# Moving GpSimd's work and the small state products of a chunked scan, and cutting the last weight loads

## Chip, cores and metric

The kernel runs on one core of one Trainium2 chip. The metric is device time in microseconds (us). The 3 runs of the kernel before gave 721.09, 721.67 and 723.37 us; the median is 721.67 us.

## What is computed

One decoder layer on 512 tokens of width 1024, in float32. One input projection feeds a state space group (16 heads, the scan below) and an attention group (16 heads with a forget gate); both are normalised, projected back and added to the input. Then a mixture of 32 gated experts follows, two for each token. Cut to what matters:

```python
proj = rmsnorm(x, norm_mix_w) @ w_in
z, xbc, dt, q, k, v, f = ...             # column ranges of proj
xbc = silu(causal_dwconv(xbc))           # X, B, C
# scan, in 4 chunks of 128 tokens
a = dt * A;  cum = cumsum(a)             # inside a chunk
decay  = exp(causal(cum_t - cum_s))
y_diag = einsum((C.B) * decay * dt, X)
states = einsum(B, exp(cum_end - cum), X * dt)
h      = exp(cum_end) * h + states       # from chunk to chunk
y_off  = einsum(C, h_in) * exp(cum)
y_ssm  = rmsnorm((y_diag + y_off + X * d_skip) * silu(z))
q, k   = rmsnorm(q), rmsnorm(k)          # per head
y_att  = rmsnorm(softmax(q.k + c_t - c_s) @ v)
x = x + concat(y_ssm, y_att) @ w_out
x = x + moe(rmsnorm(x))                  # top group of 4, 2 of its 8 experts
# expert: (silu(x@w_gate) * (x@w_up)) @ w_down, width 256
```

## The kernel before

Each engine has a program of its own, written out by hand, and semaphores tie them. TensorE (PE), VectorE (DVE), ScalarE (ACT), GpSimd (POOL) and SyncE (SP, which issues DMAs) each work through their list in order.

The projections are 60 passes of TensorE. A pass has 8 tiles (k = 0 to 7), each of 3 float32r products of 128x512, since each float32 factor is split into a high and a low part (`three`, L1402 to L1404). A block of 512 weight columns is used by four passes in a row. Its slots are loaded by SP into a ring of 6 (`raw`), ACT makes the high part (`high`), DVE the low part (`weight_low`, L282, here "a low"); SP loads a slot when the low of the slot six before is made. Seven lows follow the third pass of a block and one the fourth.

The scan runs beside the 16 passes of the q and k columns. The text counts these passes i = 0 to 15; chunk c of the scan belongs to passes 4c to 4c+3. The names:

- ACT, for each pass i: the square of the pass's result, an `Ln` and an `Exp` for the row norm, the copy of a transposed tile. After pass 4c: the copy of the products C.B (`cb_copy`), two groups of decays (`decays`, L1138, four heads each) and for c > 0 the exponential of `decay_out` (L1144), the decays on the outgoing side; after pass 4c+1 the other two groups.
- DVE, for each pass i: a sum and a scaling (`qk_sum`, `qk_scale`, L2067). After pass 4c, `m_product` of groups 0 and 1, after 4c+1 of groups 2 and 3 (L2080); then `y_add(c, 0)` and after pass 4c+2 `y_add(c, 1)` (L2089 to L2099), and after pass 4c+3 `state_keep` for both halves.
- PE: `diag(c, w)` (L1521, four products), `y_off(c, g)` (L1543), `state(c, g)` (L1556), `cb(c)` (L1531) and the transposes `qk_transpose` (L1563) stand between tiles and passes. `diag(c, 2)` writes the bank that `y_add(c, 0)` has to read out first (`y_diag`).
- POOL: the mask of the decays (`causal_decays`), `scaled_x` (X times decay, for `state`), `gate` (y times silu(z)) and `skip_term` (X times d_skip, put into `y`). One tile `y` serves all chunks: `skip_term(c+1)` works on what SP loads into `y` once `gate(c)` has read it.
- SP: `load_conv_chunk(c)` waits for `gated` of chunk c-1 and loads `y`; right behind it in SP's list stands `load_decay_out(c)`, two loads of 256 KB into `decay_out`.

The experts come in 16 pairs of two. For each pair SP streams 6 MB of weights (`gu`, `dn`). PE turns the tokens, does the gate and up products (`gate_up`, L1784, L1807, L1813), a transpose and the down products (`down`, L1842, in two column halves of 512 and two row parts q = 0, 1). The result of the last pair is added to sums that POOL gathers from the output (`gather_last_sums`) and scattered. `keep_busy(n)` are n products of constants whose result nobody reads.

## Time and profile before

| what | value |
|---|---|
| median of 3 runs | 721.67 us |
| profiled execution, its own time | 722.29 us |
| its span | 720.6 us |
| PE busy | 679.8 us (94%) |
| PE weight loads | 470.5 us (65%) |
| DVE busy | 389.4 us (54%) |
| ACT busy | 291.4 us (40%) |
| POOL busy | 132.3 us (18%) |
| mean DMA rate over the span | 226 GB/s |
| mean granted TensorE clock | 0.976 |

The span is what the profiler saw of one execution; 1.7 us of its own time lie around it. Busy PE means that a product was under way, not that it ran at its peak. In rows of the profile, "idle before <-" names what ended an engine's idle time. The passes of q and k run from about 137 to 258 us, attention to about 415 us, and the expert weights stream from about 486 us at 400 to 424 GB/s until about 705 us.

### The profile page before, as it was taken

What the parts mean: (1) busy time and instruction counts of PE and PEld (TensorE: products, weight loads), DVE (VectorE), ACT (ScalarE), POOL (GpSimd) and SP (SyncE); (2) the same over time, 40 slices, a digit from 0 to 9 for tenths busy, and PEclk for the clock granted to TensorE, in tenths of its full rate; (3) what the DMA queues carried; (4) which work ended last, traced back from release to release, by engine and by line L of the source; (5) the groups of instructions that cost most, each with busy time, mean ns of one, the idle gap of its engine ahead of it and who ended that gap; (6) DMA issues with size and microseconds to landing.
All of it is one profiled execution on the core that took longest, in us unless ns stands there. A gap on an engine that the chain in (4) does not pass through costs nothing.

```text
span 720.6 us, 10643 instructions
## 1 busy us (share of the span) xinstructions
PE 679.8 (94%) x3850; PEld 470.5 (65%) x3850; DVE 389.4 (54%) x845; ACT 291.4 (40%) x651; POOL 132.3 (18%) x167
## 2 busy tenths in 40 slices
PE   8999999999999999999999999989999978878975
PEld 7878888777777888767767788877434323323542
DVE  6866678878879665777887643471222211212211
ACT  5934534465555546665676423221212111202200
POOL 2300010114222120022223110020132321122331
PEclk9999999999999999999999999979999989989998
DMA  8333255426254343191020079689999999999993
GB/s 297 95 115 117 77 175 162 131 74 176 82 153 146 88 146 104 45 362 46 19 100 2 10 291 424 241 335 376 412 417 416 403 409 399 424 418 414 412 403 120
DMA packets 61159, 162.77 MB, mean 226 GB/s; under 512 B 14184, under 2 KB 25604, under 8 KB 49840
## 3 DMA queue, kind: packets, MB, share of 16 engines
q1 hardware_dynamic: 49120, 144.64, 53.6%
q0 software_dynamic: 6880, 9.02, 4.3%
q10 hardware_dynamic: 5104, 8.39, 3.2%
q8 instruction: 33, 0.54, 0.3%
q14 instruction: 22, 0.18, 0.1%
HBM read 157.67 MB, written 20.28 MB: 247 GB/s over the span
## 4 chain that ended last, share of the span: by engine, by line
PE 27%; DMA 9%; SPq 9%; DVE 2%; issue 2%; ACT 1%; POOL 0%; POOLq 0%; DVEq 0%; ACTq 0%
PE bank L1813 6%; DMA s_gu<-in_w_expert_gate_dram 4%; SPq L427 4%; DMA s_gu<-in_w_expert_up_dram 4%; PE bank L1842 3%; PE bank L1402 3%; PE bank L1404 3%; PE bank L1403 3%; SPq L475 2%; SPq L461 2%; PE bank L1784 2%; PE bank L1678 1%; PE bank L1635 1%; PE bank L1618 1%; PE bank L1760 1%
## 5 line engine op out<-in xcount | busy, mean ns | idle before, releaser
L1813 PE MATMUL bank<-s_gu,s_xgT 128*64 128x512 f32 x352 | 84.6, 636 | 15.8 <-DMA s_gu<-in_w_expert_up_dram 15.8
L282 DVE TENSOR_TENSOR s_wl<-s_raw,s_wh 128x512 fp32r<-128x512 f32 x116 | 91.6, 836 | 11.8 <-ACT s_wh L1019 11.5
L1019 ACT ACTIVATE s_wh<-s_raw 128x512 fp32r<-128x512 f32 x120 | 72.6, 627 | 42.1 <-PE bank L1404 18.6
L1402 PE MATMUL bank<-s_wh,s_hTh 128*128 128x512 f32 x192 | 78.7, 410 | 0.0
L1404 PE MATMUL bank<-s_wh,s_hTl 128*128 128x512 f32 x192 | 75.2, 391 | 0.0
L1403 PE MATMUL bank<-s_wl,s_hTh 128*128 128x512 f32 x192 | 74.8, 390 | 0.0
L1813 PEld LDWEIGHTS bank<-s_gu,s_xgT 128*64 128x64 f32 x352 | 28.4, 146 | 70.9 <-issue 70.9
L1318 ACT ACTIVATE s_sg<-bank,s_slot_scale 128x256 f32<-128x256 f32 x16 | 7.6, 474 | 151.7 <-PE bank L1813 104.5
L1842 PE MATMUL bank<-s_dn,s_hidT 128*64 128x512 f32 x256 | 58.5, 598 | 1.6 <-DVE s_hidT L2385 1.6
L2385 DVE COPY s_hidT<-bank 128x256 f32<-128x256 f32 x16 | 6.8, 424 | 92.9 <-PE bank L1822 92.9
L2418 DVE SCALAR_TENSOR_TENSOR s_yrow<-bank,s_slot_scale,s_xg 128x512 f32<-128x512 f32 x30 | 21.2, 746 | 46.4 <-PE bank L1842 46.4
L1402 PEld LDWEIGHTS bank<-s_wh,s_hTh 128*128 128x128 f32 x192 | 36.1, 188 | 10.1 <-issue 2.8
L895 POOL DMA_INDIRECT s_xg<-x_rows,s_slot_rows x16 | 16.6, 1038 | 140.0 <-DVE s_yrow L2418 105.3
L1404 PEld LDWEIGHTS bank<-s_wh,s_hTl 128*128 128x128 f32 x192 | 36.0, 188 | 7.9
L1403 PEld LDWEIGHTS bank<-s_wl,s_hTh 128*128 128x128 f32 x192 | 36.1, 188 | 7.5 <-issue 0.7
L1402 PE MATMUL bank<-s_hTh,s_wh 128*128 128x512 f32 x96 | 39.2, 409 | 0.0
L1404 PE MATMUL bank<-s_hTh,s_wl 128*128 128x512 f32 x96 | 37.7, 392 | 0.0
L1403 PE MATMUL bank<-s_hTl,s_wh 128*128 128x512 f32 x96 | 37.4, 389 | 0.0
L1842 PEld LDWEIGHTS bank<-s_dn,s_hidT 128*64 128x64 f32 x256 | 17.0, 136 | 31.2 <-issue 27.1
L1190 ACT ACTIVATE s_Pe<-s_Pe,s_nmax 128x512 f32<-128x512 f32 (+3 forms) x41 | 22.6, 554 | 25.1 <-DVE s_nmax L2167 25.1
L2039 DVE SCALAR_TENSOR_TENSOR s_acc<-s_up,s_cvec,s_acc 128x512 f32<-128x512 f32 x36 | 28.7, 797 | 1.3
L775 POOL TENSOR_SCALAR_AFFINE_SELECT s_decay_rows<-s_decay_rows 128x2048 f32<-128x2048 f32 x4 | 8.5, 2121 | 107.2 <-DMA s_decay_rows<-decay_rows 107.2
(307 smaller groups left out, 1372.2 us busy)
## 6 DMA issues: line engine op xcount, KB each, us to landing
s_dn<-in_w_expert_down_dram SPq DMA_DIRECT2D x28, 1024.0 KB
s_gu<-in_w_expert_gate_dram SPq DMA_DIRECT2D x26, 1024.0 KB
s_gu<-in_w_expert_up_dram SPq DMA_DIRECT2D x24, 1024.0 KB, 30.2
s_raw<-in_w_in_dram SPq DMA_DIRECT2D x88, 256.0 KB, 4.4
s_raw<-in_w_out_dram SPq DMA_DIRECT2D x32, 256.0 KB, 3.4
s_gu<-in_w_expert_up_dram SPq DMA_DIRECT2D x12, 512.0 KB
s_decay_rows<-decay_rows SPq DMA_DIRECT2D x4, 1024.0 KB, 4.6
s_gu<-in_w_expert_gate_dram SPq DMA_DIRECT2D x8, 512.0 KB
```

Source lines behind the costliest of these rows:

```text
L282: eng.tensor_tensor(low, full, high.bitcast(F32), ALU.subtract).then_inc(sem(f"{what}_low_{low_engine(what, i)}"), 1)
L427: sp.dma_start(m[f"gu{b}"][:, half, which, :, :].rearrange("p k f -> p (k f)"), src).then_inc(sem(f"gu_in{b}"), 16)
L895: pool.indirect_dma_start(out=token_rows(p), out_offset=None, in_=x2_dram[:, :], in_offset=bass.IndirectOffsetOnAxis(ap=slot_rows[:, p:p + ...
L1019: act.activation(wh[:, i % HL, :], raw[:, i % RAW, :], ACT.Copy).then_inc(sem("w_high"), 1)
L1190: act.activation(p_tile(v), p_tile(v), ACT.Exp, bias=nmax[:, v:v + 1], scale=-1.0, accum_out=rsum[:, v:v + 1]).then_inc(sem("p_exp"), 1)
L1402: pe.matmul(dst, ah, bh, start=start, stop=False)
L1403: pe.matmul(dst, ah, bl, start=False, stop=False)
L1404: return pe.matmul(dst, al, bh, start=False, stop=stop)
L1813: last = pe.matmul(ps[j][r, :].rearrange("p (w f) -> p w f", w=2), m["xgT"][:, j, k, r], gu[:, half, :, k, :], start=(k == 0), stop=(k == ...
L1842: last = pe.matmul(ps[6 + nb][r, :], m["hidT"][:, j, at:at + CAP], dn[:, half, q, nb * BLK:(nb + 1) * BLK], start=(q == 0), stop=(q == 1))
L2039: ins = dve.scalar_tensor_tensor(out=a, in0=up[:, f % 2, t:t + T], scalar=tap[t], in1=a, op0=ALU.mult, op1=ALU.add)
L2418: dve.scalar_tensor_tensor(out=m["yrow"][:, j, cols], in0=ps[6 + nb][:], scalar=gates, in1=token_rows(p)[:, cols], op0=ALU.mult, op1=ALU.a ...
```

## The change

Five edits in the scan and three at the end:

- PE: the first `cb(0)` stands two tiles later. `diag(c, 0)` and `diag(c, 1)` stand behind tiles 2 and 4 of pass 4c+2 (before: 1 and 3). `diag(c, 2)` and `diag(c, 3)`, which stood side by side at the boundary behind pass 4c+2, stand behind tiles 1 and 3 of pass 4c+3, and `y_off(c, 1)` behind tile 4 of it.
- POOL: `skip_term(c + 1)` stands ahead of `scaled_x(c + 1)`. `scaled_x(c)` waits for the chunk's last `m_product`. `gate(c)` waits for `state_keep(c, 1)`, and in the last chunk for the last `qk_sum`.
- DVE: the copies of `y` onto itself in chunk 0 are gone (`y_diag` of chunk 0 takes the place of `y_whole`, whose counts fall by 2), and the scaling of `dte` stands behind the first two `m_product`.
- ACT: the first square stands ahead of the table load, and the two exponentials for `dte` and `etot` behind the first decays.
- SP: the counts of `y_whole` follow; no load moves in its list.
- End: `keep_busy(5)` stands between the down products of pair 14 and the gate products of pair 15; the second row part of the last down weights comes as four loads of 256 KB (columns 0 to 511 of both experts, then 512 to 1023) instead of two of 512 KB, and the last down product of all waits for the last two alone (`last_columns_in`).

```diff
@@ load_last_down
-            for q in range(2):
+            for half in range(2):
+                src = w_expert_down[0][p + half * NPAIR].rearrange("(p k) n -> p k n", p=P)[:, 0, :]
+                sp.dma_start(m[f"dn{p % NDN}"][:, half, 0, :], src).then_inc(sem(f"dn_in{p % NDN}"), 16)
+            for nb in range(2):
+                cols = slice(nb * BLK, (nb + 1) * BLK)
                 for half in range(2):
-                    src = w_expert_down[0][p + half * NPAIR].rearrange("(p k) n -> p k n", p=P)[:, q, :]
-                    sp.dma_start(m[f"dn{p % NDN}"][:, half, q, :], src).then_inc(sem("last_down_in" if q else f"dn_in{p % NDN}"), 16)
+                    src = w_expert_down[0][p + half * NPAIR].rearrange("(p k) n -> p k n", p=P)[:, 1, cols]
+                    sp.dma_start(m[f"dn{p % NDN}"][:, half, 1, cols], src).then_inc(sem("last_columns_in" if nb else "last_down_in"), 16)
@@ load_decay_out, load_first_bias
-                sp.wait_ge(sem("y_whole"), 2 * c)
+                if c == 1:
+                    sp.wait_ge(sem("y_diag"), 2)
+                else:
+                    sp.wait_ge(sem("y_whole"), 2 * (c - 1))
...
-                sp.wait_ge(sem("y_whole"), 2 * TC)
+                sp.wait_ge(sem("y_whole"), 2 * (TC - 1))
@@ POOL
                 if c < TC - 1:
+                    pool.wait_ge(sem("m_done"), 4 * c + 4)
                     if c:
                         pool.wait_ge(sem("state_done"), 2 * c)
...
-                pool.wait_ge(sem("y_whole"), 2 * c + 2)
+                if c:
+                    pool.wait_ge(sem("y_whole"), 2 * c)
+                else:
+                    pool.wait_ge(sem("y_diag"), 2)
+                if c < TC - 1:
+                    pool.wait_ge(sem("state_kept"), 2 * c + 2)
+                else:
+                    pool.wait_ge(sem("qk_sum"), 16)
...
                 gate(c)
+                skip_term(c + 1)
                 scaled_x(c + 1)
-                skip_term(c + 1)
@@ ACT
+            qk_square(0)
             act.preload_act_table_set("natural_log_exp_and_others")
-            act.wait_ge(sem("steps_known"), 4)
-            act.activation(dte[:], dte[:], ACT.Exp).then_inc(sem("dt_acts"), 1)
-            act.activation(etot[:], tot[:, :, 0:H], ACT.Exp).then_inc(sem("dt_acts"), 1)
...
                     if i:
                         decay_out_exp(i // 4)
+                    else:
+                        act.wait_ge(sem("steps_known"), 4)
+                        act.activation(dte[:], dte[:], ACT.Exp).then_inc(sem("dt_acts"), 1)
+                        act.activation(etot[:], tot[:, :, 0:H], ACT.Exp).then_inc(sem("dt_acts"), 1)
@@ PE
-                    if i == 1 and k == 1:
+                    if i == 1 and k == 3:
                         cb(0)
-                    if i >= 2 and i % 4 == 2 and k in (1, 3):
-                        diag(i // 4, k // 2)
+                    if i >= 2 and i % 4 == 2 and k in (2, 4):
+                        diag(i // 4, k // 2 - 1)
+                    if i >= 2 and i % 4 == 3 and k in (1, 3):
+                        diag(i // 4, 2 + k // 2)
+                    if i > 4 and i % 4 == 3 and k == 4:
+                        y_off(i // 4, 1)
...
-                if step == 1:
-                    if c:
-                        y_off(c, 1)
-                    diag(c, 2)
-                    diag(c, 3)
...
+                    elif final and q:
+                        pe.wait_ge(sem("last_columns_in"), 32)
...
                 down(p, p)
+                if p == NPAIR - 2:
+                    keep_busy(5)
@@ DVE
-                else:
-                    dve.tensor_copy(y[:, cols], y[:, cols]).then_inc(sem("y_whole"), 1)
...
-                if i == 0:
-                    dve.wait_ge(sem("dt_acts"), 5)
-                    dve.tensor_tensor(dte[:], dte[:], sp[:, :, 0:H], ALU.mult).then_inc(sem("scales_known"), 1)
-                    dve.wait_ge(sem("scales_known"), 1)
...
                     m_product(c, 1)
+                    if c == 0:
+                        dve.wait_ge(sem("dt_acts"), 5)
+                        dve.tensor_tensor(dte[:], dte[:], sp[:, :, 0:H], ALU.mult).then_inc(sem("scales_known"), 1)
+                        dve.wait_ge(sem("scales_known"), 1)
```

What stands in a row on POOL from the mask of chunk 1 to the gating of chunk 1, before (`s_decay_rows` the mask, `s_zs` the gating, `s_Xs` the scaled X, `s_y` the skip term):

```order
L763 TENSOR_TENSOR s_Xs<-s_X,s_dte 128x1024 [waits x_silu,x_rows,scales_known]
L775 AFFINE_SELECT s_decay_rows<-s_decay_rows 128x2048 [waits cum_rows_moved]
L770 TENSOR_TENSOR s_zs<-s_y,s_zs 128x1024 [waits z_stored,y_whole]
L763 TENSOR_TENSOR s_Xs<-s_X,s_dte 128x1024 [waits state_done]
L755 TENSOR_TENSOR s_y<-s_y,s_dskip_of 128x1024 [waits conv_chunk_in]
L775 AFFINE_SELECT s_decay_rows<-s_decay_rows 128x2048 [waits cum_rows_moved]
```

and now:

```order
L771 TENSOR_TENSOR s_Xs<-s_X,s_dte 128x1024 [waits x_silu,m_done,x_rows,scales_known]
L790 AFFINE_SELECT s_decay_rows<-s_decay_rows 128x2048 [waits cum_rows_moved]
L785 TENSOR_TENSOR s_zs<-s_y,s_zs 128x1024 [waits z_stored,state_kept,y_diag]
L762 TENSOR_TENSOR s_y<-s_y,s_dskip_of 128x1024 [waits conv_chunk_in]
L771 TENSOR_TENSOR s_Xs<-s_X,s_dte 128x1024 [waits state_done,m_done]
L790 AFFINE_SELECT s_decay_rows<-s_decay_rows 128x2048 [waits cum_rows_moved]
```

The skip term moved ahead of the scaled X, the gating waits for the kept state, and the scaled X for the m products.

What stands on TensorE behind pass 4c+2 of chunk 1, before (`s_qn` the transpose, `s_BC,s_Hst` is `y_off`, `s_M,s_X` is `diag`, the 512 wide ones are tiles of the pass):

```order
L1563 MATMUL bank<-s_ident,s_qn 128x128 x3
L1543 MATMUL bank<-s_BC,s_Hst 128x128 [waits state_kept,y_off_scaled]
L1543 MATMUL bank<-s_BC,s_Hst 128x128 x3
L1521 MATMUL bank<-s_M,s_X 64x128 [waits y_diag,m_done]
L1521 MATMUL bank<-s_M,s_X 64x128 x3
L1521 MATMUL bank<-s_M,s_X 64x128 [waits m_done]
L1521 MATMUL bank<-s_M,s_X 64x128 x3
L1402 MATMUL bank<-s_wh,s_hTh 128x512 [waits qk_scaled]
L1403 MATMUL bank<-s_wl,s_hTh 128x512
```

and now, the tiles left out where a line of dots stands:

```order
L1581 MATMUL bank<-s_ident,s_qn 128x128 x3
L1420 MATMUL bank<-s_wh,s_hTh 128x512 [waits qk_scaled]
...
L1422 MATMUL bank<-s_wh,s_hTl 128x512
L1539 MATMUL bank<-s_M,s_X 64x128 [waits y_diag,m_done]
L1539 MATMUL bank<-s_M,s_X 64x128 x3
L1420 MATMUL bank<-s_wh,s_hTh 128x512
...
L1539 MATMUL bank<-s_M,s_X 64x128 [waits m_done]
L1539 MATMUL bank<-s_M,s_X 64x128 x3
...
L1561 MATMUL bank<-s_BC,s_Hst 128x128 [waits state_kept,y_off_scaled]
L1561 MATMUL bank<-s_BC,s_Hst 128x128 x3
L1420 MATMUL bank<-s_wh,s_hTh 128x512
```

The two groups of `diag` and the `y_off` left the boundary and stand alone among the tiles of the pass behind it.

## Rows read from the trace of the kernel before

**Rows 1.** The chain that ended last (start us, us, what), its last long transfer.
```profile
667.26 31.48 DMA s_gu<-in_w_expert_gate_dram
```

**Rows 2.** TensorE's waits: line, who, us in total, times, longest.
```profile
PE bank L1521 <- DVE s_y L2089: 0.8, 1, 0.8
PE bank L1563 <- DVE s_qn L2067: 0.7, 1, 0.7
PE bank L1521 <- DVE s_M L2080: 0.6, 1, 0.6
PE bank L1531 <- ACT s_BC L1085: 0.6, 1, 0.6
PE bank L1543 <- DVE s_decay_out L2095: 0.4, 1, 0.4
```

**Rows 3.** Timeline of TensorE around the small products (start us, us, engine, line, op).
```profile
198.76 0.39 PE L1404 MATMUL bank<-s_wh,s_hTl 128*128 128x512 f32 x1
...
203.53 0.39 PE L1404 MATMUL bank<-s_wh,s_hTl 128*128 128x512 f32 x1
...
210.14 0.39 PE L1404 MATMUL bank<-s_wh,s_hTl 128*128 128x512 f32 x1
...
211.94 0.40 PE L1403 MATMUL bank<-s_wl,s_hTh 128*128 128x512 f32 x1
...
212.86 0.40 PE L1404 MATMUL bank<-s_wh,s_hTl 128*128 128x512 f32 x1
...
214.12 0.39 PE L1403 MATMUL bank<-s_wl,s_hTh 128*128 128x512 f32 x1
...
218.83 0.60 PE L1563 MATMUL bank<-s_ident,s_qn 128*128 128x128 f32 x4
...
249.71 0.39 PE L1404 MATMUL bank<-s_wh,s_hTl 128*128 128x512 f32 x1
...
252.72 0.39 PE L1403 MATMUL bank<-s_wl,s_hTh 128*128 128x512 f32 x1
```

**Rows 4.** Timeline of VectorE in the scan.
```profile
137.76 1.28 DVE L282 TENSOR_TENSOR s_wl<-s_raw,s_wh 128x512 fp32r<-128x512 f32 x2
...
161.08 9.99 DVE L282 TENSOR_TENSOR s_wl<-s_raw,s_wh 128x512 fp32r<-128x512 f32 x7
...
205.07 0.69 DVE L2112 TENSOR_TENSOR s_Hst<-s_Hst,bank 128x512 f32<-128x512 f32 x1
...
218.33 0.68 DVE L2089 TENSOR_TENSOR s_y<-s_y,bank 128x512 f32<-128x512 f32 x1
```

**Rows 5.** Timeline of GpSimd: the gating of chunk 1.
```profile
193.05 2.78 POOL L770 TENSOR_TENSOR s_zs<-s_y,s_zs 128x1024 f32<-128x1024 f32 x1 [1.36 <-DVE s_y L2097]
```

**Rows 6.** Timeline of SyncE's queue: the two loads of chunk 2.
```profile
198.04 0.38 SPq L574 DMA_DIRECT2D s_y<-conv_rows  x1
198.46 1.59 SPq L580 DMA_DIRECT2D s_decay_out<-decay_rows  x2
```

**Rows 7.** Tile s_decay_out, issue to landing of its loads.
```profile
DMA to landing us min/median/max: 6.3/7.3/8.7
```

**Rows 8.** Tile s_y, issue to landing of its loads.
```profile
DMA to landing us min/median/max: 3.9/6.7/8.0
```

**Rows 9.** Timeline of ScalarE: the exponential of chunk 2's outgoing decays.
```profile
211.59 1.05 ACT L1144 ACTIVATE s_decay_out<-s_decay_out 128x1024 f32<-128x1024 f32 x1
```

**Rows 10.** Timeline of TensorE: constant products, gate and up products of pairs 13 and 15.
```profile
481.94 3.78 PE L1746 MATMUL bank<-s_wr,s_ones 128*128 128x144 f32 x16
...
670.23 7.08 PE L1807 MATMUL bank<-s_gu,s_xgT 128*64 128x256 f32 x64
...
698.88 8.81 PE L1807 MATMUL bank<-s_gu,s_xgT 128*64 128x256 f32 x64 [2.36 <-DMA s_gu<-in_w_expert_gate_dram]
```

**Rows 11.** Windows at the end: us, busy of each engine, TensorE clock, DMA share, GB/s.
```profile
701.00:702.00 1.00, 1.00 (x8) 0.69 (x6) 0.00 (x0) 0.00 (x0) 0.77 (x1) 0.50 1.00 401
...
709.00:710.00 1.00, 0.66 (x4) 0.34 (x6) 0.29 (x1) 0.00 (x0) 0.00 (x0) 1.00 0.71 271
```

More of the change, by code:

```diff
@@ L1156, in y_square @@
                 act.activation(Pe[:, 0:2, :].rearrange("p a t -> p (a t)"), zs[:, c, :], ACT.Square).then_inc(sem("y_squared"), 1)
+            qk_square(0)
             act.preload_act_table_set("natural_log_exp_and_others")
-            act.wait_ge(sem("steps_known"), 4)
-            act.activation(dte[:], dte[:], ACT.Exp).then_inc(sem("dt_acts"), 1)
-            act.activation(etot[:], tot[:, :, 0:H], ACT.Exp).then_inc(sem("dt_acts"), 1)
             for i in range(16):
                 n = N_QK + i
-                qk_square(i)
+                if i:
+                    qk_square(i)
                 qk_rstd(i)
```

## Prediction

> **What bounds the kernel now.** I read the busy shares first: TensorE is busy 94% of the span, so a gain has to shorten its list or take away its idle time. Then the chain that ended last: its last long piece is a transfer of gate weights that takes 31.48 us to land, at 698.7 us [rows 1]. From about 486 us the expert weights stream without a gap, and the time is when that stream starts plus its length plus the tail behind it. What the scan gains or loses moves the start of the stream by the same amount, since its loads wait for TensorE's passes behind the scan. So there are two places, the scan (137 to 260 us) and the last 15 us.
>
> Third, TensorE's waits by line. In the scan they are few: 0.8 us for VectorE's read-out of the bank (`diag(0, 2)`), 0.7 us for a scaled q tile, 0.6 us for the first m product, 0.6 us for B and C, 0.4 us for `y_off(2, 1)` [rows 2]. Together 3.1 us; that is all that moving work about can win in the scan. Last, the timelines of all engines in the scan, to see which of them is late next.
>
> **Scan: what goes.** The 0.6 for B and C goes, since `cb(0)` stands two tiles later. A tile is 3 products: from 198.76 to 203.53 there are 21 starts, 0.227 us each, so a tile is 0.68 us and the two are 1.36. The 0.6 for the first m product goes likewise (one tile later, and the scaled X no longer runs beside it). The 0.8 goes because the bank is now asked for 1.36 us behind the boundary. The 0.7 came from seven lows that took 9.99 us while POOL worked; two lows without it take 1.28, 0.64 each [rows 4]. POOL's gating and scaled X leave that place, the lows take about 5 us, and the wait goes. The 0.4 goes, as `y_off` is asked for later. I take all: -3.1 us. The two copies of `y`, 0.4 us each, stood on VectorE where nothing waited for them but that: nothing more.
>
> **Scan: what the splitting costs.** A group of `diag` alone between two tiles costs 0.81 us: from the last start before it (212.86) to the second behind it (214.12) is 1.26, less two starts of 0.227. At the boundary the same sum gives 2.56 for transposes, `y_off` and two groups (249.71 to 252.72), and 1.35 for transposes and `y_off` (210.14 to 211.94), so two groups side by side cost 1.21 [rows 3]. Two alone cost 1.62, 0.41 more, in each of 4 chunks: +1.6 us. `y_off(c, 1)` alone isn't shown; each group paid 0.2 for standing alone, I take the same, 3 times: +0.6. Bounds 0 and twice that. Sum +2.2 us.
>
> The Trainium skill, "TensorE: Matmul & The Clock Gate", section "Step-by-step: what each phase is for", says that TensorE pulls a weight load ahead of products in flight, so that the next tile's weights load under the present one. By that a group in the middle of a pass would cost no more than at a boundary, and the sum would be 2.2 us less. The trace speaks against it at this place, with 0.81 against 0.6.
>
> **Scan: the new wait.** `gate(c)` waited for `y` alone and now waits for `state_keep(c, 1)`. Behind it hangs a row of work: SP loads the next `y` only when the gating is done; behind that load in SP's list stand the two loads of `decay_out`; ScalarE needs these for its exponential behind the decays of pass 4c; and behind that exponential on ScalarE stand the square of pass 4c+1, its `Ln` and `Exp`, and the last two groups of decays. Take chunk 2, which hangs on chunk 1's gating:
> - Now the gating of chunk 1 begins at 193.05 and takes 2.78 [rows 5]. The last addition to the state stands at 205.07 and ends at 205.76 [rows 4]. In the change the lows in front of it start later (they follow `y_add(1, 1)`, which needs products now inside the pass), but run at 0.64 instead of beside POOL. The two nearly cancel; I take 0.6 earlier, 205.15. The gating ends at 207.95, against 195.83.
> - SP issues the load of `y` at 208.0, and `decay_out` 0.42 and some 1.2 behind it, by the spacing of [rows 6]. These land 6.3 to 8.7 us after their own issue [rows 7], so between 7.5 and 9.1 after the load of `y`. I take 8.1: 216.1.
> - ScalarE's exponential, 1.05 long, started at 211.59 without a wait [rows 9]; it now starts at about 216.1. That is 4.5 late, and so is the square behind it, the decays behind that and the m products from them.
> - `y_add(2, 0)` stood at 218.33 and took 0.68 [rows 4]; it frees the bank at 219.0 + 4.5 = 223.5. TensorE reaches the boundary at 218.83 [rows 3], spends 0.60 on the transposes and 1.36 on two tiles, and asks for the bank at 220.8. It waits 2.7 us, in part at the transposes of pass 9, whose scaling is late too.
>
> Chunk 3 has the same shape, hangs on chunk 2's gating, and costs the same: 2.7. Chunk 1 hangs on chunk 0's, whose state is only copied, with fewer steps in front of it; its bounds are 0 and 2.7 and I take 1.1. Sum +6.5 us. What is queued on POOL itself behind the held gating (skip term, scaled X) has time: the scaled X is needed three passes later.
>
> Bounds. If the loads landed as fast as chunk 0's `y`, which took 3.9 us alone [rows 8], the last one would be in 1.2 + 3.9 = 5.1 after the load of `y`, 3.0 earlier, and the wait would be gone: 0 instead of 6.5. With the slowest, 9.1, each of the three waits is 1.0 longer: 9.5. I stay near the middle of the rows for this very pair of loads, because what slows them is each other and the load of `y`, and those still run together.
>
> Scan: -3.1 + 2.2 + 6.5 = +5.6 us.
>
> **The end.** Before pair 15's gate products TensorE was idle for 2.36 us, and its 64 products then took 8.81, against 7.08 for pair 13 [rows 10]. In that stretch the granted clock was 0.50, the 1.2 GHz level [rows 11]; ahead of the fall stood that idle time. Five constant products fill it: eight took 3.78, so five take at most 2.36, just the gap, and do not delay the gate products. I expect the clock to stay at 2.4 GHz and 1.7 us to go here. Not all of it arrives: at 709 to 710 the last down weights were still moving, at 271 GB/s [rows 11], and the second row part can't start before they land. The four smaller loads let the first column half go with half of them landed, and VectorE's last two operations of 0.75 us each begin earlier. I take -1.1 us, between 0 (the clock falls all the same, or the weights set the end) and -1.7.
>
> **Sum.** The profiled execution took 722.29 us by its own clock, 0.6 above the median of the runs. +5.6 - 1.1 = +4.5, so 726.8 by that execution and 726.2 us by the median of 721.67. With the bounds of the landing time (and of the end) the likeliest case alone reaches from 722.5 to 730.
>
> **Rivals.**
> - *The loads land in time.* For it: with the gating later, no weight loads stand in front of `y` and `decay_out` in the DMA engines, and chunk 0's `y` landed in 3.9. Against it: the pair now takes 6.3 at least. It decides if they land within about 5 us after the load of `y`. Then -3.1 + 2.2 - 1.1 = -2.0: 719.7 us, not slower. A chance of 0.2.
> - *Standing alone costs nothing.* The sum is then +5.6 - 2.2 - 1.1 = +2.3: 724.0 us. For it: on the whole TensorE loads weights under its products. Against it: the 0.81 of [rows 3]. 0.1. By the rule of the Trainium skill on weight loads (above) this would be the case.
> - *The waits feed each other.* A late pass makes the lows late, these the kept state, and that the next chunk's gating. Then chunk 3 pays for chunk 2's wait again, with the slow landing of 9.1: 9.5 of waits instead of 6.5 and nothing at the end, 721.7 - 3.1 + 2.2 + 9.5 = 730.3 us. Against it: all of these are counted from TensorE's own passes, so a wait shifts the next chunk and does not add to it. 0.1.
>
> My forecast has 0.6. About 0.3% (2.2 us) is what a measurement of this kernel can tell from no change. Below 719.5 lies half of the first rival, and its meeting with the second: 0.14. Within 2.2 us lie the other half and the near ends of the forecast and of the second: 0.2. The rest, 0.66, is slower. The range of 8 in 10 takes in the first rival at its near end and stops short of the third: 719.7 to 729.5.
>
> **What would show it.** In the new profile: ScalarE idle in front of `decay_out`'s exponential, released by its load, about 3 to 6 us in each of three chunks; POOL's gating of chunks 0 to 2 right behind the last `s_Hst` operation; TensorE waiting at `diag(c, 2)` for `s_y`, some 2 us for chunks 2 and 3, and at a transpose for `s_qn`; the seven lows in about 5 us. The waits of [rows 2] for B and C and for the first m product gone. At the end the 64 products of pair 15 in about 7.1 us at the full clock. The prediction is wrong if ScalarE doesn't wait for `decay_out`: then the scan is level or faster, and the time is near 720.

## The result, and the profile after

| kernel | median us | runs | lowest to highest |
|---|---|---|---|
| before | 722.56 | 8 | 721.09 to 724.34 |
| changed | 725.20 | 8 | 724.14 to 727.29 |

The ratio is 1.0038, with a 95% interval of 1.0024 to 1.0053: slower by 1.7 to 3.8 us. Forecast was 726.2 in a range of 719.7 to 729.5. The profiled execution of the changed kernel took 727.29 us by its own clock (span 725.7); it was the slowest of the eight. So its lengths are read stage by stage, and each is tied to the kernels run later. One of the six runs of `e9_pairs` (below) fell into a slower state, 765.57 us, and is left out of its median.

TensorE's waits in the scan (line, who, us in total, times, longest), against [rows 2]:

```profile
PE bank L1539 <- DVE s_y L2110: 4.3, 3, 1.9
PE bank L1581 <- DVE s_qn L2088: 0.6, 2, 0.4
```

All five waits of [rows 2] are gone, and a new one is there, at `diag(c, 2)` for VectorE's read-out of the bank: 0.45, 1.92 and 1.92 us in chunks 1 to 3. Ahead of it stands what the prediction named. The rows are ScalarE's exponentials of the outgoing decays ([rows 9] had no idle time in front), then GpSimd's gating of chunk 1 and SyncE's loads behind it (start us, us, engine, line, op; [rows 5] and [rows 6] before):

```profile
179.09 1.06 ACT L1159 ACTIVATE s_decay_out<-s_decay_out 128x1024 f32<-128x1024 f32 x1 [4.30 <-DMA s_decay_out<-decay_rows]
...
212.14 1.06 ACT L1159 ACTIVATE s_decay_out<-s_decay_out 128x1024 f32<-128x1024 f32 x1 [4.84 <-DMA s_decay_out<-decay_rows]
...
247.13 1.06 ACT L1159 ACTIVATE s_decay_out<-s_decay_out 128x1024 f32<-128x1024 f32 x1 [5.40 <-DMA s_decay_out<-decay_rows]
```
```profile
202.35 2.84 POOL L785 TENSOR_TENSOR s_zs<-s_y,s_zs 128x1024 f32<-128x1024 f32 x1 [11.11 <-issue]
```
```profile
205.28 0.38 SPq L578 DMA_DIRECT2D s_y<-conv_rows  x1
205.70 1.27 SPq L587 DMA_DIRECT2D s_decay_out<-decay_rows  x2
```

The gating ends at 205.19, the load of `y` goes out at 205.28, that of `decay_out` at 205.70, and ScalarE gets it at 212.14, 4.84 us after it was free. The landing line of tile `s_decay_out` in the same profile, against 6.3/7.3/8.7 in [rows 7]:

```profile
DMA to landing us min/median/max: 5.0/5.6/6.4
```

What the prediction doesn't have stands behind the wait. TensorE's timeline across it in chunk 2 (the start of each product is what counts), then windows of 1 us (busy of each engine, granted clock, DMA share, GB/s):

```profile
217.41 0.40 PE L1422 MATMUL bank<-s_wh,s_hTl 128*128 128x512 f32 x1
219.72 0.66 PE L1539 MATMUL bank<-s_M,s_X 128*64 128x128 f32 x8 [1.92 <-DVE s_y L2110]
220.31 0.58 PE L1420 MATMUL bank<-s_wh,s_hTh 128*128 128x512 f32 x1
220.68 0.63 PE L1421 MATMUL bank<-s_wl,s_hTh 128*128 128x512 f32 x1
221.11 0.63 PE L1422 MATMUL bank<-s_wh,s_hTl 128*128 128x512 f32 x1
...
224.58 0.40 PE L1422 MATMUL bank<-s_wh,s_hTl 128*128 128x512 f32 x1
```
```profile
219.00:220.00 1.00, 0.28 (x6) 0.31 (x8) 0.96 (x2) 0.00 (x0) 0.94 (x1) 1.00 0.95 385
220.00:221.00 1.00, 1.00 (x10) 0.75 (x6) 0.97 (x2) 0.00 (x0) 0.96 (x1) 0.80 1.04 426
221.00:222.00 1.00, 1.00 (x4) 0.72 (x4) 1.00 (x2) 0.00 (x0) 0.00 (x0) 0.50 0.36 148
222.00:223.00 1.00, 1.00 (x5) 0.35 (x3) 0.39 (x2) 0.83 (x3) 0.60 (x1) 0.50 0.00 0
...
224.00:225.00 1.00, 1.00 (x7) 0.86 (x6) 0.69 (x1) 1.00 (x3) 0.40 (x1) 0.99 0.00 0
```

After 1.92 us of idle time the granted clock is 0.50 from about 220.6 to 224.0, the 1.2 GHz level, and products start 0.43 us apart instead of 0.23. The same happens behind the wait of chunk 3 (255 to 258 us).

The whole of it can be read from start to start. From the tile in front of `diag(c, 2)` to the start of `y_off(c, 1)` this kernel takes 7.40 us in chunk 2 (217.41 to 224.81) and 7.41 in chunk 3 (252.40 to 259.81). The same list of products takes 3.89 us in both chunks of `e1_decay_first` (below), where TensorE doesn't wait there. So each of the two waits of 1.92 us costs 3.5 us of TensorE's time.

VectorE's lows, against the 9.99 us for seven in [rows 4]: one group of six and the seventh.

```profile
159.89 4.28 DVE L282 TENSOR_TENSOR s_wl<-s_raw,s_wh 128x512 fp32r<-128x512 f32 x6
164.56 0.69 DVE L282 TENSOR_TENSOR s_wl<-s_raw,s_wh 128x512 fp32r<-128x512 f32 x1 [0.40 <-ACT s_wh L1034]
```

5.4 us from the first start to the last end; forecast was about 5. The end (TensorE, then VectorE), against [rows 10]:

```profile
701.22 1.49 PE L1763 MATMUL bank<-s_wr,s_ones 128*128 128x144 f32 x10
703.67 7.13 PE L1824 MATMUL bank<-s_gu,s_xgT 128*64 128x256 f32 x64 [0.96 <-DMA s_gu<-in_w_expert_gate_dram]
...
712.78 3.65 PE L1861 MATMUL bank<-s_dn,s_hidT 128*64 128x512 f32 x16 [0.85 <-DMA s_dn<-in_w_expert_down_dram]
```
```profile
716.08 1.41 DVE L2437 SCALAR_TENSOR_TENSOR s_yrow<-bank,s_slot_scale,s_xg 128x512 f32<-128x512 f32 x2 [3.68 <-DMA s_xg<-out_dram,s_slot_rows]
```

Five constant products take 1.49 us, the 64 products of pair 15 take 7.13 instead of 8.81, and then VectorE's last operations wait for the gathered sums, which is new: the chain that ended last now comes through this transfer and not through the down products.

```profile
710.95 4.94 DMA s_xg<-out_dram,s_slot_rows
```

**A measure for the scan.** From the start of the transposes of the last B/C block (136.97 us in the kernel before) to the start of those behind pass 16 (263.91). Both ends stand at the same place in every kernel here, so the difference is the scan's alone. Each value comes from one profiled execution. How far two executions of the same list differ, two rows of the table show: the kernel before and `e2_end_only` have the same scan and differ by 0.63 us, the changed kernel and its repeat by 0.42. Before and after, and all kernels:

```profile
136.97 0.49 PE L1446 MATMUL bank<-s_ident,s_BC 128*128 128x128 f32 x3
...
263.91 0.60 PE L1563 MATMUL bank<-s_ident,s_qn 128*128 128x128 f32 x4
```
```profile
136.33 0.60 PE L1464 MATMUL bank<-s_ident,s_BC 128*128 128x128 f32 x4
...
269.02 0.55 PE L1581 MATMUL bank<-s_ident,s_qn 128*128 128x128 f32 x3 [0.17 <-DVE s_qn L2088]
```

| kernel | scan us | against before | median us | ratio (95%) |
|---|---|---|---|---|
| before | 126.94 | | 722.05 to 722.56 in four sets | |
| changed | 132.69 | +5.75 | 725.20 | 1.0038 (1.0024 to 1.0053) |
| e10_again: changed, once more | 132.27 | +5.33 | 726.30 | 1.0047 (1.0032 to 1.0062) |
| e1_decay_first: changed, `decay_out` loaded ahead of `y` | 124.54 | -2.40 | 718.81 | 0.9954 (0.9941 to 0.9968) |
| e11_warm: changed, the two long waits filled | 128.94 | +2.00 | 723.51 | 1.0009 (0.9993 to 1.0026) |
| e7_gate_free: changed, gating not held | 128.72 | +1.78 | 723.16 | 1.0014 (1.0002 to 1.0027) |
| e6_unsplit_only: changed, TensorE's order of before | 131.90 | +4.96 | 725.70 | 1.0055 (1.0035 to 1.0076) |
| e4_split_only: before, TensorE's order of the change | 133.64 | +6.70 | 729.39 | 1.0103 (1.0086 to 1.0119) |
| e5_decay_first_unsplit | 123.52 | -3.42 | 718.28 | 0.9947 (0.9932 to 0.9963) |
| e8_cb_late: e5 with B and C late | 123.15 | -3.79 | 717.45 | 0.9928 (0.9915 to 0.9941) |
| e9_pairs: e8 with two groups side by side | 122.44 | -4.50 | 717.79 | 0.9923 (0.9906 to 0.9939) |
| e12_old_end: e8 without the edits of the end | 123.23 | -3.71 | 717.96 | 0.9939 (0.9919 to 0.9959) |
| e2_end_only: before with the edits of the end | 127.57 | +0.63 | 721.91 | 0.9992 (0.9982 to 1.0002) |

### The profile page after: what moved, and what is told of

It reads as the page before. It is cut to its first block and busy times, and to the rows that moved or that the text cites. A ratio compares the mean times of both kernels' runs of the same rounds, so it can differ in the third digit from the quotient of the medians.

```text
span 725.7 us, 10669 instructions
## 1 busy us (share of the span) xinstructions
PE 680.9 (94%) x3860; PEld 470.4 (65%) x3860; DVE 375.0 (52%) x843; ACT 289.0 (40%) x651; POOL 131.1 (18%) x167
## 5 line engine op out<-in xcount | busy, mean ns | idle before, releaser
L1830 PE MATMUL bank<-s_gu,s_xgT 128*64 128x512 f32 x352 | 82.8, 625 | 17.1 <-DMA s_gu<-in_w_expert_up_dram 17.1
L1034 ACT ACTIVATE s_wh<-s_raw 128x512 fp32r<-128x512 f32 x120 | 70.7, 625 | 48.0 <-DMA s_raw<-in_w_in_dram 24.0
L282 DVE TENSOR_TENSOR s_wl<-s_raw,s_wh 128x512 fp32r<-128x512 f32 x116 | 78.5, 722 | 13.2 <-ACT s_wh L1034 13.1
L1420 PE MATMUL bank<-s_wh,s_hTh 128*128 128x512 f32 x192 | 80.6, 420 | 0.0
L2060 DVE SCALAR_TENSOR_TENSOR s_acc<-s_up,s_cvec,s_acc 128x512 f32<-128x512 f32 x36 | 27.1, 752 | 1.3
L1420 PE MATMUL bank<-s_wh,s_syTh 128*128 128x512 f32 x64 | 27.4, 428 | 0.0
```

The lines of the kernel that those rows point to most:

```text
L282: eng.tensor_tensor(low, full, high.bitcast(F32), ALU.subtract).then_inc(sem(f"{what}_low_{low_engine(what, i)}"), 1)
L1034: act.activation(wh[:, i % HL, :], raw[:, i % RAW, :], ACT.Copy).then_inc(sem("w_high"), 1)
L1420: pe.matmul(dst, ah, bh, start=start, stop=False)
L1830: last = pe.matmul(ps[j][r, :].rearrange("p (w f) -> p w f", w=2), m["xgT"][:, j, k, r], gu[:, half, :, k, :], start=(k == 0), stop=(k == ...
L2060: ins = dve.scalar_tensor_tensor(out=a, in0=up[:, f % 2, t:t + T], scalar=tap[t], in1=a, op0=ALU.mult, op1=ALU.add)
```

## The experiments

Two theories stood at first. One: SyncE's list, where the load of `decay_out` stands behind a load that waits for the held gating, makes ScalarE and then TensorE late. The other: the products moved into passes, and what VectorE then does later, make TensorE late.

**Swap the two loads** (the changed kernel)
```diff
-                    load_conv_chunk(i // KC - 6)
                     load_decay_out(i // KC - 6)
+                    load_conv_chunk(i // KC - 6)
```


> The changed kernel with one swap: SP issues the two loads of decay_out ahead of the load of y, so they no longer stand behind the wait for the held gating. Theory (the new wait hangs on that order): ScalarE's waits in front of the exponential of decay_out, 4.30, 4.84 and 5.40 us in the changed kernel, shrink to under 0.5 us each; TensorE's three waits for s_y (4.3 us together) and for s_qn (0.6) nearly go, and the slow stretch behind the last of them too: 5.0 to 6.5 us less than the changed kernel, about 719.5 us. Rival 1 (the lateness is VectorE's, from the moved lows and the held kept state): ScalarE's waits go but TensorE still waits at diag(c, 2): less than 2 us won, 723 to 725. Rival 2 (the load of y takes over as the last to land): TensorE waits at the x transposes or the y products instead, and 1 to 3 us are won.

718.81 us, 6.4 under the changed kernel (6.1 by the ratios 1.0038 and 0.9954) and faster than before. ScalarE starts the same exponential without idle time, 5.0 us earlier, and TensorE has one wait of 0.2 us left. The granted clock is 1.00 throughout the scan. ScalarE and TensorE in this kernel:

```profile
207.10 1.05 ACT L1159 ACTIVATE s_decay_out<-s_decay_out 128x1024 f32<-128x1024 f32 x1
```
```profile
PE bank L1581 <- DVE s_qn L2088: 0.2, 1, 0.2
```

SyncE now issues `decay_out` at 195.61, since the y of the chunk before is whole by then, and `y` at 205.19. The first theory holds and rivals 1 and 2 fall: the gating is as late as in the changed kernel, and nothing waits for it.

**TensorE's order alone** (the kernel before with the changed `for i in range(17)` loop and nothing else)
```diff
-                    if i == 1 and k == 1:
+                    if i == 1 and k == 3:
                         cb(0)
-                    if i >= 2 and i % 4 == 2 and k in (1, 3):
-                        diag(i // 4, k // 2)
+                    if i >= 2 and i % 4 == 2 and k in (2, 4):
+                        diag(i // 4, k // 2 - 1)
+                    if i >= 2 and i % 4 == 3 and k in (1, 3):
+                        diag(i // 4, 2 + k // 2)
...
```


> The kernel before with TensorE's order of the changed kernel alone: diag, the second y_off and the product of B and C stand inside passes. Theory (a small group alone costs 0.81 where two side by side cost 1.21): +1.6 for 4 groups of two, nothing or +0.6 for y_off, less the waits for B and C (0.6) and for the bank (0.8): +0.2 to +0.8 us against the kernel before. Rival 1 (standing alone costs nothing): -1.4 us. Rival 2 (the later products make y_add late and with it the next chunk's gating, load and exponential): +1.5 to +3 us, with waits for decay_out in front of its exponential on ScalarE.

A miss: 729.39 us, 6.9 slower than before. Its price of standing alone is the one expected (groups of 0.80 us). What it adds is waits for VectorE:

```profile
PE bank L1563 <- DVE s_qn L2066: 4.3, 5, 1.3
PE bank L1531 <- DVE s_Hst L2111: 1.3, 2, 0.7
```
```profile
195.34 0.69 DVE L2096 TENSOR_TENSOR s_y<-s_y,s_decay_out 128x512 f32<-128x512 f32 x1
195.95 8.16 DVE L282 TENSOR_TENSOR s_wl<-s_raw,s_wh 128x512 fp32r<-128x512 f32 x7
```

VectorE ends the y additions of chunk 1 at 196.03 (0.69 us from 195.34), where before it was 192.96, because the products they need now stand inside the pass. Then come the seven lows, which take 8.16 us beside GpSimd's gating and scaled X, as the 8.21 they took before (192.88 to 201.09). What is behind them, the scaling of q and the kept state, comes late by the same 3 us. In the kernel before only one of these places had a wait, of 0.7 us [rows 2], so the room there was smaller than 3 us. Rival 2 named this lateness but undersized it, and expected waits for `decay_out` on ScalarE; its exponentials have no idle time in this kernel.

**Swap the loads, and TensorE's order of before** (the edits of the first run, and those of the second undone)

> The changed kernel with decay_out loaded ahead of y (as in the run beside it) and with TensorE's order of the kernel before. Theory: the split costs 1.6 to 2.2 us and saves waits of 1.4 to 2.0 (B and C, the bank, the first m product), so this one is within 0.6 us of the run with the swap alone. Rival 1 (standing alone costs nothing): 1.5 to 2 us slower than the run with the swap alone. Rival 2 (the waits saved are gone anyway by POOL's new places, since the lows run undisturbed): 1 to 2 us faster.

718.28, 0.5 under the swap alone, as the theory has it: the scan is 1.02 us shorter (123.52 against 124.54). The split costs 1.5 us and saves the wait for B and C, which is here, and is TensorE's only one:

```profile
PE bank L1549 <- ACT s_BC L1100: 0.7, 1, 0.7
```

**TensorE's order of before, loads not swapped**

> The changed kernel with TensorE's order of the kernel before (diag, y_off and the product of B and C stand where they stood); the loads of decay_out still stand behind the load of y. Theory (the wait hangs on the held gating alone): ScalarE still waits 3 to 5 us in each of three chunks for decay_out; but TensorE asks for the y products of the second half, and VectorE adds them, in the order of before, and the scan is 4 to 6 us longer than in the run of this order with decay_out first (718.28): 722 to 725. Rival 1 (the wait comes from holding and splitting together, since the split delays the kept state): ScalarE's waits are under 2 us each and the time is below 720. Rival 2 (this order is less forgiving, bank and transposes wait in a row): 726 or more.

725.70, 0.7 over what the theory gave and no better than the changed kernel. The wait has moved to `y_off(c, 1)`:

```profile
PE bank L1561 <- DVE s_decay_out L2117: 6.0, 3, 3.0
```

ScalarE waits 3.56, 3.21 and 5.04 us in front of its three exponentials, so rival 1 falls. The wait hangs on the held gating in front of the load, and not on the split. The load's place costs 8.4 us of scan here (131.90 against 123.52) and 8.15 with the changed order (132.69 against 124.54); the split costs 1.0 with the swap and 0.8 without it, which is little more than two executions of one scan differ by.

This run also shows that the length of a wait does not settle what the clock does behind it. TensorE's three waits here last 1.71, 1.28 and 3.01 us. Behind the first the granted clock falls to 0.50 (189 to 192.4 us); behind the second and behind the third, the longest of all, it stays at 1.00, and the tiles start 0.23 us apart:

```profile
187.68 1.16 PE L1561 MATMUL bank<-s_BC,s_Hst 128*128 128x128 f32 x8 [1.71 <-DVE s_decay_out L2117]
```
```profile
190.00:191.00 1.00, 1.00 (x7) 0.65 (x4) 0.96 (x2) 0.58 (x2) 1.00 (x1) 0.50 0.07 16
```
```profile
255.04 1.16 PE L1561 MATMUL bank<-s_BC,s_Hst 128*128 128x128 f32 x8 [3.01 <-DVE s_decay_out L2117]
...
257.49 0.39 PE L1421 MATMUL bank<-s_wl,s_hTh 128*128 128x512 f32 x1
257.72 0.39 PE L1422 MATMUL bank<-s_wh,s_hTl 128*128 128x512 f32 x1
```

From the tile in front of the transposes to the second product behind the groups, less two starts, the third place took 5.84 us and the same place without a wait 2.56. So 3.01 us of waiting cost 3.3 us here, less than the 3.5 that 1.92 us cost in the changed kernel. Why the clock fell behind waits of 1.71 and 1.92 us and not behind this one is not shown.

**The gating not held**
```diff
-                if c < TC - 1:
-                    pool.wait_ge(sem("state_kept"), 2 * c + 2)
-                else:
-                    pool.wait_ge(sem("qk_sum"), 16)
```


> The changed kernel with the gating of all four chunks no longer held until the kept state: it starts when y of the chunk is whole, and the loads of y and decay_out behind it start some 7 to 10 us sooner; it runs beside VectorE's lows again. Theory: ScalarE's waits for decay_out go (under 0.5 us each), and what comes in their place is VectorE's lows stretched from 0.7 to 2.4 us beside the gating, three in each chunk: 4 to 5 us of VectorE per chunk, of which TensorE sees 0.4 to 1.3 us as a wait for s_qn at the transposes. 719.5 to 722.5, so 0.5 to 3.5 over the run with decay_out first. Rival 1 (the stretched lows cost TensorE nothing, the hold is for nothing): 718.8, as that run. Rival 2 (they cost as much as in the kernel before with TensorE's new order alone, which was 6.9 us slower than before): 725 to 729.

723.16, 0.7 over the upper end of the theory. ScalarE's waits are gone, and the lows are slow again: seven take 6.45 us, where six and a seventh took 3.69 and 0.69 with the gating held.

```profile
192.69 6.45 DVE L282 TENSOR_TENSOR s_wl<-s_raw,s_wh 128x512 fp32r<-128x512 f32 x7
```
```profile
PE bank L1545 <- DVE s_Hst L2127: 1.3, 2, 0.7
PE bank L1577 <- DVE s_qn L2084: 1.2, 1, 1.2
```
```profile
192.72 3.69 DVE L282 TENSOR_TENSOR s_wl<-s_raw,s_wh 128x512 fp32r<-128x512 f32 x6
196.77 0.69 DVE L282 TENSOR_TENSOR s_wl<-s_raw,s_wh 128x512 fp32r<-128x512 f32 x1 [0.36 <-ACT s_wh L1034]
```

The stops cost more than the 2.9 us of waiting (2.5 in these rows, 0.4 for a low), since the 0.66 us of each wait for `s_Hst` stands in a place that took 2.15 us instead of 0.90. Held or not held is 4.2 us of scan (124.54 against 128.72), once `decay_out` doesn't stand behind it. Against the kernel with TensorE's order alone (133.64) this one is 4.9 us shorter. There the scaled X too ran beside the lows; whether that is all of the 4.9 no run tells apart from the other small moves. The moves on GpSimd, with the small ones on ScalarE and VectorE that belong to them, and with `decay_out` put ahead, are thus worth 9.1 us of scan in that order of TensorE (133.64 against 124.54), and the place of one load turned the sign of the whole.

The Trainium skill, "SBUF — State Buffer", section "SBUF: two separate sides", says that VectorE and GpSimd share a pair of SBUF ports: between an operation of VectorE with two SBUF inputs and one of GpSimd that reads SBUF, the one that starts first has the pair for the whole instruction and the other waits. The rows agree. The gating starts at 192.85 us, 0.16 behind the first low, and takes 2.72; seven lows of 0.61 are 4.3 us and took 6.45, so they stood still for 2.15 of it.

**B and C late, and two groups side by side** (both on the swap with TensorE's order of before)
```diff
-                    if i == 1 and k == 1:
+                    if i == 1 and k == 3:
                         cb(0)
```


> The changed kernel with decay_out first and TensorE's order of before, but the product of B and C two tiles later, as in the changed kernel. Theory (its wait of 0.71 us for s_BC, 0.98 with what the stop costs, goes and nothing comes in its place): 0.7 to 1.0 us less than the run without this (718.28), about 717.4. Rival (the wait moves to the first m product or the transposes of pass 1): no difference.

717.45, 0.8 less, inside what was expected. But a wait of 0.6 for `s_y` in chunk 0 appeared, so the scan gained 0.37 only, and the rest of the 0.8 is within what such medians move.

```diff
-                    if i >= 2 and i % 4 == 2 and k in (1, 3):
-                        diag(i // 4, k // 2)
+                    if i >= 2 and i % 4 == 2 and k == 3:
+                        diag(i // 4, 0)
+                        diag(i // 4, 1)
```


> The run beside this (decay_out first, TensorE's order of before, B and C late), with the first two diag groups of a chunk side by side in the middle of pass 4c+2 instead of two tiles apart. Theory (a group alone costs 0.80 us, two side by side 1.22): 4 times 0.38, so 1.5 us less than the run beside it, about 715.9. Rival 1 (standing alone costs nothing): no difference. Rival 2 (the third m product needs the first group's M buffer, so it is 1.4 us later, and with it diag(c, 2) and y): a wait at diag(c, 2) of 0.3 to 0.8 us in each chunk takes back most of it.

The scan is 0.71 shorter, half of what was expected, and the time is the same (717.79 against 717.45, intervals that overlap). Side by side the two groups take their 1.22 us:

```profile
180.37 0.39 PE L1422 MATMUL bank<-s_wh,s_hTl 128*128 128x512 f32 x1
180.68 1.09 PE L1539 MATMUL bank<-s_M,s_X 128*64 128x128 f32 x16
...
181.71 0.50 PE L1420 MATMUL bank<-s_wh,s_hTh 128*128 128x512 f32 x1
182.04 0.40 PE L1421 MATMUL bank<-s_wl,s_hTh 128*128 128x512 f32 x1
```

From 180.37 to 182.04 are 1.67 us, less two starts of 0.227. But at the next boundary the same products took 2.72 instead of 2.56 in each of three chunks, and chunk 0 waits 0.91 for the bank instead of 0.59. Together these give back 0.8 of the 1.5. Rival 2 expected a wait at `diag(c, 2)` in each chunk; only chunk 0 has one. The price of standing alone is shown place by place, and about half of it is given back here.

**The clock behind the wait** (the changed kernel, and beside it the changed kernel as it is)
```diff
+                    if i in (11, 15) and k == 1:
+                        for _ in range(6):
+                            pe.matmul(ps[6][:, 0:P], ones[:], ident[:], start=True, stop=True)
                     if i >= 2 and i % 4 == 3 and k in (1, 3):
                         diag(i // 4, 2 + k // 2)
```


> The changed kernel once more, for a second profile and on the same chip as the run with constants in front of diag(c, 2). Theory (its scan always loses the clock after the two waits of 1.9 us): scan again 5 to 6 us longer than before, time 725.2. Rival (the clock falls in some executions only, the first profile showed a bad one): the scan of this profile is 3 to 4 us longer than before, with the granted clock at 1.00 behind one or both waits.

> The changed kernel with six constant products (128x128, into a bank that the scan doesn't use) ahead of diag(2, 2) and diag(3, 2), in the place where TensorE is idle for 1.92 us. Theory (behind each of these two waits TensorE runs at the 1.2 GHz level for some 3 us and this costs 1.3 to 1.6 us beside the wait itself): the waits stay, filled, and the granted clock stays at 1.00: 2.6 to 3.3 us less than the changed kernel, about 722.3. Rival 1 (the slow products behind the wait are slow for another reason, such as late weights): no difference. Rival 2 (the six products take longer than the wait): up to 1 us slower than the theory.

The changed kernel repeats: 726.30, scan 132.27, waits of 1.91 and 1.92 and the clock at 0.79 over 218 to 226 us. With the constant products the clock stays:

```profile
218.00:226.00 8.00, 6.84 (x37) 5.13 (x38) 5.47 (x9) 3.59 (x8) 3.91 (x2) 0.79 0.37 131
252.00:260.00 8.00, 6.08 (x33) 4.22 (x32) 5.47 (x12) 4.26 (x11) 0.00 (x0) 0.79 0.00 0
```
```profile
218.00:226.00 8.00, 7.61 (x53) 6.08 (x52) 6.85 (x13) 4.12 (x10) 3.91 (x2) 1.00 0.36 131
252.00:260.00 8.00, 7.42 (x51) 5.82 (x50) 6.36 (x11) 4.11 (x9) 0.00 (x0) 1.00 0.01 2
```

723.51, 2.8 less than its neighbour; the scan is 3.3 shorter than its neighbour's and 3.75 shorter than in the first profile. TensorE can't go on earlier, it only does something meanwhile. From start to start as above, the two places take 5.69 and 5.89 us here, against 7.40 and 7.41 in the first profile of the changed kernel, 7.39 and 7.44 in the second and 3.89 without a wait. So of the 3.5 us that each wait of 1.92 us costs, 1.5 to 1.7 are the lower clock, and 1.8 to 2.0 are the stop. Both rivals fall. In the repeated profile and in this one chunk 1 has no wait at the bank, so the 0.45 of the first profile is not in every execution, and the 0.50 that it cost there is no part of the clock's price.

**The end**, first in the kernel before, then taken out of the fastest kernel (both edits of the end, as the change has them)

> The kernel before with the two edits of the end alone: five constant products ahead of pair 15's gate products, and the last down weights in six loads. Theory (the prediction's end term, -1.1, corrected by the changed kernel's trace): the gate products of pair 15 take 7.1 us instead of 8.8, and then the gathered rows of the merge set the end: 0.8 to 1.3 us less than before, the rest of the 1.7 lost in VectorE's wait for s_xg. Rival 1 (the constants don't hold the clock in the kernel before, its gate weights land earlier than in the changed one): no difference. Rival 2 (nothing caps it): 1.7 us less.

> The fastest kernel so far (decay_out first, TensorE's order of before, B and C late: 717.45) without the two edits of the end. Theory (the gate products of pair 15 take 1.7 us more at the lower clock, of which the gathered rows of the merge hide the greater part): 0.4 to 1.0 us slower, about 718.1. Rival 1 (the whole 1.7 shows): 719.1. Rival 2 (the gate weights are there in time in this kernel, so the clock doesn't fall): no difference.

0.6 us less (interval -1.3 to +0.1) in the one, 0.5 less in the other (717.45 against 717.96): the first under what the theory gave, the second inside it, and neither alone is told from nothing. In e12_old_end the gate weights were there in time in the profiled execution, and the products took 7.27 us without a fall of the clock (rival 2's condition); so the constants had nothing to save in it. The last down products wait 1.02 us for their weights, but VectorE waits longer, until 708.29, for the gathered sums, and these are what the chain that ended last comes through:

```profile
694.87 7.27 PE L1821 MATMUL bank<-s_gu,s_xgT 128*64 128x256 f32 x64
...
706.77 1.94 PE L1856 MATMUL bank<-s_dn,s_hidT 128*64 128x512 f32 x8 [1.02 <-DMA s_dn<-in_w_expert_down_dram]
```
```profile
708.29 1.41 DVE L2430 SCALAR_TENSOR_TENSOR s_yrow<-bank,s_slot_scale,s_xg 128x512 f32<-128x512 f32 x2 [4.54 <-DMA s_xg<-out_dram,s_slot_rows]
```

So no profile here gives a cause for the 0.5, and it may be nothing.

In e2_end_only they take 7.13 and VectorE then waits 3.67 us for the gathered sums, as in the changed kernel.

## Why the prediction was right, point by point

The time was inside the range and the mechanism is the forecast's own. That the scan's sum came out so near (+5.6 against +5.75) is in part luck: the waits that go were worth 1.3 us more than the step gave, the new wait cost 1.65 more, and the two errors have opposite signs. The medians moved by 2.6 us, 1.9 less than the +4.5 of the forecast.

- *The waits that go, -3.1.* All went, and they were worth -4.4. The step took the us that the waits last [rows 2], not what their places cost from start to start, by the sum of [rows 3]. In the kernel before, the place of the 0.73 us wait for `s_qn` took 2.04 us where the same place without it takes 0.90; likewise 1.29 for 0.45 at B and C. By this count over the five waits (and one place of 0.27 without a listed wait) the stops cost 4.4. (The kernel before was profiled once more in `e2_end_only`, with waits of 1.0, 0.9, 0.8, 0.6 and 0.4 us and a scan 0.63 longer, so this term isn't the same in every execution.) The kernel with the swap and TensorE's order of before shows the same: -3.4, with the 1.0 of B and C still in it.
- *The splitting, +2.2.* A group alone is 0.80 us in over a dozen places, two side by side 1.22 (2.56 less 1.34), four times 0.38 is 1.5, against 1.6 in the step. `y_off` alone took 0.90 us; in the row at the boundary it is 2.56 - 1.67 = 0.89. Its +0.6 was wrong: nothing. And 0.4 for a last small wait for `s_qn` came to it. With the swap the scan is 4.4 - 1.5 - 0.4 = 2.5 shorter by this count, and 2.40 in the profile. The second rival falls for `diag`: two groups apart cost 0.38 us more than side by side, in every kernel here. For `y_off` it holds. The rule of the Trainium skill on weight loads ("TensorE: Matmul & The Clock Gate", named in the prediction) isn't borne out at the groups of `diag`.
- *The new wait, +6.5.* The waits themselves were 0.45, 1.92 and 1.92 at the bank and 0.41 at a transpose, where the steps gave 1.1, 2.7 and 2.7. The gating of chunk 1 started at 202.35, not 205.15, because of two things that the step had nearly cancelling: the y additions of chunk 1 ended no later than before (the waits in front had gone), and the seven lows behind them took 4.75 us (192.80 to 197.55) and not 8.21.

  But TensorE was 3.1 us ahead by then as well (it started the transposes of pass 9 at 215.76; 218.83 in [rows 3]), so the earlier gating made its wait no shorter. The exponential stood 6.95 us behind the gating's end, not 8.1: with the gating later, the loads landed in 5.0 to 6.4. The step took the middle of [rows 7] because the pair and the load of `y` slow each other and still run together. They do in the changed kernel too. What is gone there are four weight loads right in front: in `e7_gate_free`, where SyncE issues them from 193.40 to 197.69 us and the load of `y` behind them, the pair lands in 6.5 to 8.1, and in `e1_decay_first`, with the weight loads in front but `y` not, in 4.8 to 6.1. In these profiles it took both to make them slow.

  The whole term was 8.15 (132.69 against 124.54). By places it is 3.51 and 3.52 for the two waits of 1.92, 0.50 for the one of 0.45 and 0.62 for the one at the transposes. In the first two about 3.2 us are the lower clock (7.03 less the 1.80 and 2.00 that stay in `e11_warm`); the rest, about 4.9, are the waits with their stops. The step had no clock in it, though the same prediction saw the clock fall behind an idle 2.36 us at the end.
- *Scan, +5.6.* 5.75 in the one profile and 5.33 in the other.
- *The end, -1.1.* The clock stayed, as said, and the products lost 1.7 us. But the cap was not the down weights, it was the gathered sums, and 0.5 to 0.8 of it arrive by the medians and ratios: 0.6 in e2_end_only, and 0.8 between the ratios 0.9939 and 0.9928 of kernels in which the clock did not fall either way. None of these is told from nothing, so how much of the term is real stays open.
- *The sum, +4.5.* The profiled execution was 5.0 over that of before, but the medians differ by 2.6, and in the second measurement by 4.3 (3.4 by the ratio). The profiled execution was at the top of its runs both times (727.29 and 727.55). Whether the other executions lose less in the scan or later isn't shown: no profile fell on one. A hint is that the mean granted clock was 0.974 in the two slowest runs of `e10_again` (727.50 and 727.55 us) and 0.977 to 0.979 in its four fastest (724.41 to 724.69 us), as if the clock fell less in these. That stays open.
- *Rivals.* The loads did not land in time: the last came 6.9 us after the load of `y` went out (205.28 to 212.14), where 5 were needed; and the waits did not feed each other: they are 1.92 in chunk 2 and 1.92 in chunk 3.

Two things were not in the prediction at all. Alone, the split costs 6.9 us, since it uses up the room that VectorE had beside GpSimd; in the change GpSimd's moves hide that. And held gating is worth 4.2 us of scan, if the one load behind it is put ahead. The kernel with that, and with TensorE's order of before but for the later product of B and C, runs at 717.45 us, 0.72% under the kernel before.

## What to carry to other kernels

When an operation is held back, look at what stands behind the transfer that waits for it in the queue, and move ahead of it whatever doesn't need it. Price a wait of TensorE by the place it stands in (start before to start behind), not by its length, and look at the granted clock behind it: it fell behind the four waits of 1.9 us of the changed kernel and behind one of 1.71, and did not behind one of 3.01. A group of `diag` put alone into a pass cost 0.2 us more here, a `y_off` nothing; and products moved so make whoever reads their bank late by as much as they were moved.

## What the runs showed of the hardware

- VectorE's subtraction from SBUF to SBUF (128x512, f32) takes 0.61 to 0.69 us, and seven of them 6.45 to 9.99 us while GpSimd works on SBUF too. An operation with a bank as one input kept its time: beside GpSimd's scaled X (219.06 to 220.96 us in the changed kernel) the product of `decay_out` with its bank took 0.69, and the addition from SBUF to SBUF behind it, started at 220.33, took 1.17 where it takes 0.69 alone.
- A stop of TensorE costs more than its wait, by an amount that depends on the products behind it: 0.73 us of waiting at transposes took 1.14 us of time, 0.57 at the product of B and C 0.84, 0.60 at a group of `diag` 0.67, without a fall of the clock in the windows.
- The clock fell behind 1.9 us of idle time in four places of two profiles of the changed kernel (218 to 226 and 252 to 260 us), and stayed at 1.00 where six constant products stood there, with 0.39 and 0.58 us of idle time behind them. In e6_unsplit_only it fell behind 1.71 us and not behind 1.28 or 3.01.
- The two loads of `decay_out` landed 4.8 to 6.1 us after their issue with four weight loads right in front (e1_decay_first), 5.0 to 6.4 with the load of `y` in front (the changed kernel), and 6.5 to 8.1 with both (e7_gate_free).
